# Rotary embedding read straight from PSUM in the last projection stage, with four rotating banks and context tiles prepared one unit sooner

## The reference

```
hx = modulate(rms_norm_2(x, norm_g[i]), shift_x, scale_x)
hc = modulate(rms_norm_2(ctx, norm_g[i]), shift_c, scale_c)
qx, kx, vx, gx = split(hx @ w_in)      # 1024, 256, 256, 1024 columns
qc, kc, vc, gc = split(hc @ w_in)      # of these only kc and vc are used here
qx = rope_axial(qx, ang_r, ang_c)
kx = rope_axial(kx, ang_r, ang_c)

def rope_1d(x, ang):                   # on each half of the 64 features of a head
    x1, x2 = split(x, 2)
    return concat([x1 * cos - x2 * sin, x2 * cos + x1 * sin])
```

## Time and profile before

| What | us |
|---|---|
| median of 3 runs | 1643.08 |
| fastest, slowest run | 1640.40, 1643.74 |
| the profiled execution, whole time | 1644.63 |
| its span (first to last instruction) | 1642.5 |
| of it around the span | 2.13 |
| PE busy, DVE busy, ACT busy, POOL busy | 1566.6, 987.7, 750.5, 502.8 |

### The profile page before, as it was taken

One profiled execution on the slowest core, in us unless ns is written; L12 is line 12 of the kernel. 1 busy time (PEld: TensorE's weight loads), 2 busy tenths in 40 slices (PEclk: granted clock), 3 DMA queues, 4 the chain that ended last, 5 costly groups with the idle time before them and its releaser, 6 DMA issues.

```text
span 1642.5 us, 23420 instructions
## 1 busy us (share of the span) xinstructions
PE 1566.6 (95%) x8264; PEld 1222.0 (74%) x8264; DVE 987.7 (60%) x2254; ACT 750.5 (46%) x1413; POOL 502.8 (31%) x231
## 2 busy tenths in 40 slices
PE   7998999999899999999899999999999988999998
PEld 5886666678688888888777787778777767865566
DVE  6236555365689867646656756666675366147854
ACT  6225766634343323244334554445454432247753
POOL 3651332245244444444121211111114442330012
PEclk9999999999899999999799999999999989999998
DMA  6850121263256565633111111111111121220001
GB/s 199 182 151 33 59 65 71 103 232 134 90 204 193 186 202 189 199 120 103 39 52 39 41 38 46 43 38 38 38 39 52 39 79 64 77 65 14 1 14 64
DMA packets 48400, 149.33 MB, mean 91 GB/s; under 512 B 5782, under 2 KB 9110, under 8 KB 48184
## 3 DMA queue, kind: packets, MB, share of 16 engines
q1 hardware_dynamic: 37080, 112.45, 22.2%
q10 hardware_dynamic: 11232, 35.72, 6.4%
HBM read 141.53 MB, written 6.62 MB: 90 GB/s over the span
## 4 chain that ended last, share of the span: by engine, by line
PE 81%; DVE 7%; ACT 6%; issue 5%; POOL 1%; DMA 0%; ACTq 0%; POOLq 0%; DVEq 0%
PE ps L339 40%; PE ps L343 20%; PE ps L560 4%; PE ps L571 4%; PE ps L541 3%; PE ps L1334 3%; PE ps L1298 2%; PE ps L1310 1%; PE ps L1062 1%; PE ps L407 1%; ACT w_h L324 1%; ACT sb L626 1%; DVE tg L1905 1%; DVE xn L1972 1%; POOL w_l L960 1%
## 5 line engine op out<-in xcount | busy, mean ns | idle before, releaser
L960 POOL TENSOR_TENSOR w_l<-raw,w_h 128x1024 fp32r<-128x1024 f32 (+1 forms) x190 | 455.3, 2397 | 912.0 <-ACT w_h L324 892.3
L324 ACT ACTIVATE w_h<-raw 128x1024 fp32r<-128x1024 f32 x190 | 200.5, 1057 | 367.3 <-PE ps L339 309.4
L339 PE MATMUL ps<-x2h,w_h 128*128 128x512 f32 (+1 forms) x816 | 245.9, 367 | 25.9 <-DVE x2l L1978 13.7
L339 PE MATMUL ps<-x1h,w_h 128*128 128x512 f32 x584 | 237.4, 406 | 17.4 <-POOL w_l L960 10.7
L339 PE MATMUL ps<-x2h,w_l 128*128 128x512 f32 (+1 forms) x816 | 231.8, 349 | 0.0
L343 PE MATMUL ps<-x2l,w_h 128*128 128x512 f32 (+1 forms) x816 | 231.7, 349 | 0.0
L339 PE MATMUL ps<-x1h,w_l 128*128 128x512 f32 x584 | 230.2, 394 | 0.0
L343 PE MATMUL ps<-x1l,w_h 128*128 128x512 f32 x584 | 229.4, 393 | 0.0
L339 PEld LDWEIGHTS ps<-x2h,w_h 128*128 128x128 f32 x816 | 132.5, 191 | 60.0 <-issue 24.0
L339 PEld LDWEIGHTS ps<-x2h,w_l 128*128 128x128 f32 x816 | 132.3, 191 | 20.8
L343 PEld LDWEIGHTS ps<-x2l,w_h 128*128 128x128 f32 x816 | 132.8, 191 | 19.7
(11 more groups left out here) (311 smaller groups left out, 2604.5 us busy)
## 6 DMA issues: line engine op xcount, KB each, us to landing
raw<-in_w_mlp SPq DMA_DIRECT2D x64, 512.0 KB, 3.7
mraw<-in_w_mod ACTq DMA_DIRECT2D x51, 512.0 KB, 3.8
raw<-in_w_a SPq DMA_DIRECT2D x32, 512.0 KB, 3.5
raw<-in_w_att SPq DMA_DIRECT2D x25, 512.0 KB, 11.1
raw<-in_w_b SPq DMA_DIRECT2D x20, 512.0 KB, 3.6
raw<-in_w_g SPq DMA_DIRECT2D x16, 512.0 KB, 3.6
raw<-in_w_ao SPq DMA_DIRECT2D x9, 512.0 KB, 3.6
gates<-g_stage ACTq DMA_DIRECT2D x16, 256.0 KB, 2.1
```

Source lines behind the costliest of these rows:

```text
L324: nc.scalar.activation(split(u)[0], raw[:, u % RAW], ACT.Copy).then_inc(w_hi, 1)
L339: mm = nc.tensor.matmul(o, w[:, k], xh(k), start=(first and k == k0 and wi == 0), stop=(last and k == k1 - 1 and wi == 1))
L960: nc.gpsimd.tensor_tensor(l[:, ks], raw[:, u % RAW, ks], h[:, ks].bitcast(F32), ALU.subtract).then_inc(w_lo, 1)
```

## The change

It has three parts.

1. The rotary embedding reads the projection's PSUM bank. DVE waits for the unit's end itself. It multiplies by a sine table that was shuffled once (`ropeb[:, 2]`), multiplies in place in PSUM by the cosine, shuffles the sine product, and adds. The factor -0.125 is part of both products. ACT's copies of query units are gone; of key units it copies the context columns alone.
2. Units 0 to 7 rotate over four banks (`u % 4`). A unit from 4 on waits for the rotary embedding that last used its bank, counted by the new semaphore `rot`.
3. The context tiles are made in turns 3 to 6. ACT makes its two high tiles behind the rounding of the weights instead of ahead of it; DVE makes its two low ones behind the rotary embedding. Unit 8 waits tile by tile.

```diff
-        def products(u, parts, k0=0, k1=KT, first=True, last=True):
+        def products(u, parts, k0=0, k1=KT, first=True, last=True, ready=None):
             for k in range(k0, k1):
+                if ready:
+                    ready(k)
...
         def gate_bank(u):
-            return 2 * (u % 2) if u < N_B - 4 else 6 + u % 2
+            return u % 4 if u < 8 else 2 * (u % 2) if u < N_B - 4 else 6 + u % 2
...
                 split_ready(pe, U_B + u)
-                pe.wait_ge(hb["free"], u - 1)
-                if u == 8:
-                    nm4c.wait(pe, "lo", KT)
-                products(U_B + u, b_parts(u)).then_inc(unit, 1)
+                if u >= 12:
+                    pe.wait_ge(hb["free"], u - 11)
+                elif u >= 4:
+                    pe.wait_ge(hb["rot"], u - 3 if u < 8 else (6, 8, 9, 10)[u - 8])
+                products(U_B + u, b_parts(u), ready=(lambda k: nm4c.wait(pe, "lo", k + 1)) if u == 8 else None).then_inc(unit, 1)
...
             def take_b(u):
-                if 4 <= u < 4 + KT // 2:
-                    for k in (2 * (u - 4), 2 * (u - 4) + 1):
+                unit_done(act, U_B + u)
+                split_high(act, U_B + u + 2)
+                if 3 <= u < 3 + KT // 2:
+                    for k in (2 * (u - 3), 2 * (u - 3) + 1):
                         nm4c.wait(act, "t", k + 1)
                         shift_tile(k, 1, xn2, 1).then_inc(nm4c.hi, 1)
-                unit_done(act, U_B + u)
-                split_high(act, U_B + u + 2)
                 b = u % 2
                 if u < 8:
-                    nc.scalar.activation(b_q[:, u, :], ps[:, 2 * b], ACT.Copy, scale=-0.125).then_inc(hb["free"], 1)
                     if u == 2:
                         root(act, nm4c, 4, C)
                 elif u < 10:
-                    nc.scalar.activation(b_k[:, u - 8, :], pair(b)[:, 0:SC], ACT.Copy).then_inc(hb["free"], 1)
+                    nc.scalar.activation(b_k[:, u - 8, S:SC], pair(b)[:, S:SC], ACT.Copy).then_inc(hb["ev"], 1)
...
+            done(nc.vector.stream_shuffle(ropeb[:, 2, :], sin_t[:], SHUFFLE))
+            settle(v)
+            def ctx_low(u):
+                for k in (2 * (u - 3), 2 * (u - 3) + 1):
+                    nm4c.wait(v, "hi", k + 1)
+                    low_tile(k, 1, xn2, 1).then_inc(nm4c.lo, 1)
             for u in range(N_B - 3):
-                if u == 3:
-                    invert(v, nm4c, C)
-                if 4 <= u < 4 + KT // 2:
-                    if u == 4:
+                if 3 <= u < 3 + KT // 2:
+                    if u == 3:
+                        invert(v, nm4c, C)
                         nm4c.wait(v, "r", 1)
                     else:
-                        nm4c.wait(v, "lo", 2 * (u - 4))
-                    for k in (2 * (u - 4), 2 * (u - 4) + 1):
+                        nm4c.wait(v, "lo", 2 * (u - 3))
+                    for k in (2 * (u - 3), 2 * (u - 3) + 1):
                         x_tile(k, 1, xn2, 1).then_inc(nm4c.t, 1)
-                    for k in (2 * (u - 4), 2 * (u - 4) + 1):
-                        nm4c.wait(v, "hi", k + 1)
-                        low_tile(k, 1, xn2, 1).then_inc(nm4c.lo, 1)
                 if u < 10:
-                    x = b_q[:, u, :] if u < 8 else b_k[:, u - 8, 0:S]
-                    v.wait_ge(hb["free"], u + 1)
-                    nc.vector.stream_shuffle(ropeb[:, 0, :], x, SHUFFLE)
-                    done(nc.vector.tensor_tensor(ropeb[:, 2, :], x, cos_t[:], ALU.mult))
+                    x = ps[:, gate_bank(u)]
+                    scale = -0.125 if u < 8 else 1.0
+                    unit_done(v, U_B + u)
+                    done(nc.vector.scalar_tensor_tensor(out=ropeb[:, 0, :], in0=x, scalar=scale, in1=ropeb[:, 2, :],
+                                                        op0=ALU.mult, op1=ALU.mult))
+                    done(nc.vector.scalar_tensor_tensor(out=x, in0=x, scalar=scale, in1=cos_t[:], op0=ALU.mult, op1=ALU.mult))
                     settle(v)
-                    done(nc.vector.tensor_tensor(ropeb[:, 1, :], ropeb[:, 0, :], sin_t[:], ALU.mult))
+                    done(nc.vector.stream_shuffle(ropeb[:, 1, :], ropeb[:, 0, :], SHUFFLE))
                     settle(v)
-                    done(nc.vector.tensor_tensor(x, ropeb[:, 1, :], ropeb[:, 2, :], ALU.add))
-                    settle(v)
+                    if u >= 8:
+                        v.wait_ge(hb["ev"], u - 7)
+                    nc.vector.tensor_tensor(b_q[:, u, :] if u < 8 else b_k[:, u - 8, 0:S], x, ropeb[:, 1, :],
+                                            ALU.add).then_inc(hb["rot"], 1)
+                    if 3 <= u < 3 + KT // 2:
+                        ctx_low(u)
```

More of the change, by code:

```diff
@@ L503, in build @@
         ao_mm = sem("ao_mm")
-        hb = {n: sem("hb_" + n) for n in ["ev", "rope", "free", "gt", "vt", "ve"]}
+        hb = {n: sem("hb_" + n) for n in ["ev", "rope", "rot", "free", "gt", "vt", "ve"]}
         class Attn:
@@ L1387, in _ @@
                         mm.then_inc(hb["vt"], 1)
-            pe.wait_ge(hb["free"], 16)
+            pe.wait_ge(hb["free"], 6)
             for n, u in enumerate((N_B - 2, N_B - 1)):
@@ L1399, in gates_out @@
                 if x == 0:
-                    pe.wait_ge(hb["free"], N_B - 1)
+                    pe.wait_ge(hb["free"], N_B - 11)
                 if x == A2.blk[2]:
-                    pe.wait_ge(hb["free"], N_B)
+                    pe.wait_ge(hb["free"], N_B - 10)
             A2.between_pe = gates_out
```

## The result

The changed kernel takes 1634.35 us in the median of 4 runs (1633.26 to 1636.52), the kernel before 1643.41 (1640.40 to 1643.86, 4 runs). The ratio is 0.9946, with a 95% interval of 0.9932 to 0.9960: 9.1 us less by the medians, 6.6 to 11.2 by the interval. The forecast was 1634.3. The profiled execution took 1636.52 us against 1644.63, 8.1 us less, where the sum said 8.8.

The account below looks back on a forecast made before the run. PE, busy 95% of the span, was taken as the bound, so edits elsewhere pay only where it waits. 5.34 + 2.75 + 0.62 + 0.1 = 8.8 us off the 1643.08 median gave 1634.3, range 1631 to 1639.

Parts of the forecast that it names:

- The wait at unit 8: Between units 7 and 8, PE's stop for DVE's low context tiles goes: 5.34 us gained.
- the weights of unit 7: Ahead of unit 7, PE's wait for late weights goes because ACT rounds at the unit's end: 0.62 us gained.
- Low clock: Behind the stop at unit 8, nine pairs of matmuls no longer run at half clock: 2.75 us gained.
- The spread: Reciprocal ahead of PE's spread comes earlier, no longer behind unit 2's rotary embedding: 0.1 us gained.
- Added waits: Seven more PE waits at unit 8 and rotary waits at units 4 to 11: taken as 0, bounds 0 to 0.8 us.
- Shuffled sine: One 0.74 us shuffle on DVE behind the last latent tile, while DVE waits for unit 0: costs nothing.
- ACT's copies: Eight copies of 0.57 us on ACT go; nothing gained beyond the weights.
- in-place product: Rotary product reading and writing one PSUM bank on DVE: taken as 0.69 us, from the nearest rows.
- A held rotary embedding: Rival: POOL holds the rotary embedding from PSUM too, PE stops 1.7 us in unit 8; gain 7.1, time 1636; chance 0.04.
- a falling clock: Rival: PE's clock falls for a reason other than the stop; gain 6.1 us, time 1637.0; chance 0.04.
- The slower one: Rival: slow in-place product makes unit 9 wait for unit 7's bank; at a 10 us turn 9 us slower, 1652; chance 0.04.
- The 8.1 us: DVE turn above which unit 9 would start later than before and the kernel be slower.

Follow-up runs that it names:

- stop filled earlier: Kernel before with 22 extra matmuls on PE ahead of unit 8's wait for its weights; 128.72 us from spread to scores, ratio 0.9998.
- order alone: Kernel before with only ACT's rounding first, context tiles in turns 3 to 6, DVE's low pair behind the rotary embedding; 125.03 us spread to scores, ratio 0.9968.
- the order and the tile waits together: Kernel before with the new context-tile order and unit 8 waiting tile by tile, old rotary embedding, two banks; 123.09 us spread to scores, ratio 0.9967.
- tile waits alone: Kernel before with only unit 8's waits taken tile by tile; 125.21 us from spread to scores, ratio 0.9969.
- load run: Changed kernel with three more products on DVE in each of turns 3 to 6; 124.12 us from spread to scores, ratio 0.9945.
- loaded with one wait: Changed kernel with three more DVE products in each of turns 3 to 6 and a single wait at unit 8; 131.04 us spread to scores, ratio 1.0008.

## Why the prediction was right

The mechanism was right: PE's stop at unit 8, its late weights at unit 7 and the low clock behind the stop went, and PE came to wait for nothing else. That 1634.3 was forecast and 1634.35 measured is luck to that digit. The runs of the changed kernel spread over 3 us, the sum had 8.8 us, the stage gained 8.48, and the profiled execution 8.1. On another chip the changed kernel's median was 1636.08.

*The wait at unit 8 and the weights of unit 7* were 5.34 + 0.62 us by the sum. From unit 4 to unit 8 the kernel before took 1380.06 - 1352.09 = 27.97 us, the changed one 1374.37 - 1352.49 = 21.88: 6.09, 0.13 more. Right.

*Low clock:* 2.75 by the sum, 2.67 shown by the run with the stop filled earlier.

*The spread:* 0.1 by the sum; unit 4 begins 0.23 us sooner behind the first spread (32.95 instead of 33.18).

*Added waits:* 0 by the sum. Here 0.5 us was lost that the sum has not: units 8 to 11 go at 8.48 us each instead of 8.32 (0.64 for the four; against the run with the stop filled, which began unit 8 with a slightly longer step, 0.51). It is not the seven waits, since the run of the order alone has one wait and the same pace. The balance is 6.09 + 0.23 + 2.67 - 0.51 = 8.48.

*Shuffled sine, ACT's copies, in-place product:* the shuffle ran at 1334.54 in DVE's idle time; the in-place product took 0.69 us, the nearest rows' value; the rotary embedding was not held by POOL and the low pair was. The Trainium skill's rule of the shared interface ("GPSIMD Engine Reference", Specifications) agrees with the rows: 1.58 us against 0.88. Of the two ways that the Trainium skill gives for elementwise work on a matmul's output ("VectorE: DVE Perf Modes", Rules for kernel authors), the kernel before takes the one for many operations, copying out of PSUM first. It bought nothing per instruction here: the products out of PSUM took 0.690 us, those in SBUF 0.692 where they were not held. It cost DVE the wait behind ACT, 0.95 us in each turn, and the hold of the one product.

*What the prediction did not see* is that its parts were not additive. It put the gain down to the change as a whole; the runs show that the rotary embedding out of PSUM by itself earned 8.46 us of the stage, the order and the tile waits together 8.22, and the banks nothing. The prediction's reason, a turn of DVE brought from 6.9 us to PE's period, holds for the first; it is not the only way there. I had seen POOL's late weights at unit 7 but not those at unit 8, hidden under the longer wait. It did not matter for the sum, as ACT was freed in the changed kernel, but it was worth 1.3 us in the run with the tile waits alone.

*The rivals.* A held rotary embedding and a falling clock did not come. The slower one named unit 9 and its wait for unit 7's bank; the load run stopped at that very place, for 0.84 us, at a turn of 7.3 us. The 8.1 us worked out there is no forecast of this stop: it is the turn from which the changed kernel would be slower than the one before. By the same formula PE, with unit 9 due near 1382.4, would begin to stop from a turn of 6.4 us on if unit 7's turn were as long as the others; in the load run it was not, as the load lay in turns 3 to 6 alone.

## What to carry to other kernels

When a wait of the bounding engine ends on a chain through other engines, compare that chain's turn with the bounding engine's own period: 6.9 against 5.5 us four times over was the 5.2 us stop here, and any edit that brings the turn under the period, or that takes the wait apart so that only the last tiles are late, earns the same microseconds once. Look under a long wait for a shorter one that ends second, here weights 1.2 us late, before counting on an edit that removes the long one alone. A stop of the bounding engine can cost more than its length, and where runs differ by more than the effect, measure between two marks of the trace around the edit, and say what the whole time shows beside it.

## What the runs showed of the hardware that was not expected

- Stops of PE of 5.2 and 6.7 us (idle times of the rows) were followed by a clock of half its level, for nine and six pairs of matmuls; one of 1.7 us (order alone) and one of 1.1 (tile waits alone) left it at 1.00. In between nothing was tried. The length of the last stop is not all that counts: at unit 0 of the kernel before (1323.61 us) the clock was at 0.50 behind an idle time of 2.62 us, which itself lay behind short matmuls and pauses (PE busy 7.70 of the 12.50 us from 1311 on).
- The units with context columns run at one of two paces, 8.32 or 8.48 us for 48 matmuls, with the clock at 1.00 in both. Before, loaded with one wait, and stop filled earlier had the faster; the others had the slower, of which the third pair of each tile is 0.52 or 0.53 us long instead of 0.51. The faster one came with and without a low clock ahead, the slower one with and without a stop ahead. The loaded run changed over within itself: to 0.51 at the hesitation inside unit 8 (1380.63 us) and back to 0.53 behind the stop at unit 9. So the pace belongs neither to a kernel nor to a unit; it changed once where two steps were only 0.1 us longer. What decides it stays open; it is worth 0.5 us in this stage.
- An instruction of DVE that reads and writes the same PSUM bank in place took 0.69 us for 512 columns, as one that only reads or only writes PSUM.
- Two 256-column instructions with two SBUF inputs took 0.87 us alone, and 1.58 to 2.94 us beside one of POOL's splits, depending on where in the split they began; both times they ended 0.68 us behind it.
